# Dense feed-forwards: where the third weight split of a trip stands against the wait for the gate product

## The chip, the cores and the metric

The kernel runs on one core of a Trainium2 chip. The metric is the device time of one execution in microseconds (us). Everything is float32 at the interface; the kernel builds a float32 product out of three passes of a narrower format.

## The reference, cut to what matters

Two transformer blocks run one after the other on 256 tokens of width 1024. The first has two layers (mixer, cross-attention, convolutional feed-forward), the second has two layers (mixer, then a dense feed-forward in layer 0 and eight experts in layer 1). The change touches the three dense feed-forwards:

```
# first block, both layers: hidden width 2816, a 3-tap convolution along the tokens on the gate half
u, gt = split(x @ ffn_w_in);  a = dwconv(gt, conv_w) + conv_b
out = (silu(a) * u) @ ffn_w_out
# second block, layer 0: hidden width 3584
out = (silu(t @ w_gate) * (t @ w_up)) @ w_down
```

## The kernel before, in words

The hidden width is cut into pieces of 256 (`CW`): 11 trips in each feed-forward of the first block, 14 in that of the second. A trip `i` takes three weight chunks of 1 MB each (128 x 2048 values): gate(i), up(i) and down(i). Numbered in the order in which TensorE (PE) uses them they are gate(0), up(0), gate(1), up(1), down(0), gate(2), up(2), down(1), ... (`ffn_steps`), so that gate(i+1), up(i+1) and down(i) are the chunks 3i+2, 3i+3 and 3i+4, of 48 matmuls each.

Each chunk is split before use. ScalarE (ACT) copies the loaded float32 chunk into `w_hi`, rounded (the high part, L2132, `split_high`); VectorE (DVE) subtracts that from the chunk into `ring_low` (the low part, L1475, `split_low`). PE multiplies high by high, high by low and low by high. `w_hi` has four buffers: the high part of chunk c waits until PE has done the high passes of chunk c-4 (`ffn_done`, counted on the one matmul of a chunk that stands at L744). PE waits for the low part (`ffn_lo`) before each chunk.

Between the products, per trip: for the first block DVE applies the convolution to the gate product (`form`, L1700 to L1713); ACT takes the silu (`silu_of`; L2392 in the first block, L2413 in the second, where it waits for the gate product on PE and `form` does nothing); DVE multiplies silu and up product (L1488), ACT rounds the result into `act_hi` (L2235), DVE forms `act_lo` (L1490), and PE's down(i) uses both.

Every engine runs its instructions in the order in which they are written, and a wait holds all that is queued behind it on that engine. `dense_steps` writes the order out, once for ACT and once for DVE, with three calls of `split()` in a trip: for gate(i+1), up(i+1) and down(i). The first two chunks are split before it starts.

Each call of `split()` ends with `side(d)`, which hangs a piece of other work behind the d-th split: the weights of the modulation (`ada_w`, 24 chunks of 1 MB for each layer of the second block) are scaled on ACT (`scale_part`, 8 instructions, L2218) and added down from eight to one row block on DVE (`fold_down`, L1432 to L1436, one split later than on ACT). `due` spreads 12 of them over 28 splits in each feed-forward of the first block, and 24 over 36 splits in the second. There every trip has two on each engine: on ACT behind the splits of up(i+1) (scale A below) and of down(i) (scale B), on DVE behind the low parts of down(i) (fold A) and of the next gate chunk (fold B). The `ada_w` chunks pass through three buffers (`ring_tail`); GpSimd (POOL) fetches the next one when a fold has freed its buffer (L537).

The weight chunks pass through six buffers (`ring_head`); SyncE (SP) loads them, in the order up(i), gate(i), down(i-1), each when PE has left the buffer (L448).

Of the kernel before, what the change touches and what calls it, by code (L numbers as in the profile page):

```python
# [134 lines left out]
def program(nc, io):  # L135
# [3 lines left out]
    with ExitStack() as ctx:  # L139
# [115 lines left out]
        def ring(s):  # L255
            return ring_head[:, s, :] if s < 6 else ring_tail[:, s - 6, :]
# [124 lines left out]
        def due(d, folds):  # L381

            span = 28 if folds == 12 else 36
            return d * folds // span if 0 < d <= span else folds if d > span else 0
# [11 lines left out]
        def ffn_slot(i, n):  # L396

            if i == 3 * n - 1:
                return 3 * ((n - 1) % 2) + 2
            return (0, 1)[i] if i < 2 else (3, 4, 2, 0, 1, 5)[(i - 2) % 6]  # L400

        def ffn_low(i, n):

            return w_hi[:, (i + 1) % DEPTH_HI, :] if i == 3 * n - 1 else ring_low[:, ffn_slot(i, n), :]

        def dense_steps(split_of, form, finish, n, side):

            calls = [0]

            def split():  # L410

                if calls[0] < 3 * n - 2:
                    split_of(calls[0] + 2)
                    calls[0] += 1
                    side(calls[0])

            for i in range(n):
                form(i % 2, i)
                if i < n - 1:
                    split()  # L420
                finish(i % 2, i)
                if i < n - 1:
                    split()
                split()

        @block.sync
# [911 lines left out]
        def _(dve):  # L1338
# [4 lines left out]
            def pairs(b):  # L1343
                return tiles(bank[b][:, :], 2)
# [83 lines left out]
            def fold_down(n):  # L1428

                w = tiles(ring_tail[:, n % 3, :], KD)  # L1430
                dve.wait_ge(mod_scaled, n + 1)
                v.tensor_tensor(w[:, 0:4, :], w[:, 0:4, :], w[:, 4:8, :], ALU.add).then_inc(fold_step, 1)  # L1432
                dve.wait_ge(fold_step, 2 * n + 1)
                v.tensor_tensor(w[:, 0:2, :], w[:, 0:2, :], w[:, 2:4, :], ALU.add).then_inc(fold_step, 1)  # L1434
                dve.wait_ge(fold_step, 2 * n + 2)
                v.tensor_tensor(fold(n), w[:, 0, :], w[:, 1, :], ALU.add).then_inc(folded, 1)  # L1436
# [33 lines left out]
            def split_low(which, i, n, order=None):  # L1470

                dve.wait_ge(ffn_hi, ffn_base[which] + (i if order is None else order) + 1)
                if i == 3 * n - 1:
                    dve.wait_ge(ffn_done, ffn_base[which] + i + 2 - DEPTH_HI)
                v.tensor_tensor(ffn_low(i, n), ring(ffn_slot(i, n)), w_hi[:, i % DEPTH_HI, :].bitcast(F32), ALU.subtract).then_inc(ffn_lo, 1)  # L1475

            def dense(which, form, n, first, folds):

                def side(d):

                    for k in range(due(d - 2, folds), due(d - 1, folds)):
                        fold_down(first + k)

                def finish(p, i):

                    dve.wait_ge(up_full[p], f.next(up_full[p]))
                    dve.wait_ge(silu_ready[p], f.next(silu_ready[p]))
                    v.tensor_tensor(act[:, p, :, :], silu[:, p, :, :], pairs(2 * p + 1), ALU.mult).then_inc(f.count(product_ready[p]), 1)  # L1488
                    dve.wait_ge(act_hi_ready[p], f.next(act_hi_ready[p]))
                    v.tensor_tensor(act_lo[:, p, :, :], act[:, p, :, :], act_hi[:, p, :, :].bitcast(F32), ALU.subtract).then_inc(f.count(act_ready[p]), 1)  # L1490

                dense_steps(lambda i: split_low(which, i, n), form, finish, n, side)

            for j, tokens_in in enumerate((first_in, second_in)):
                dve.wait_ge(tokens_in, f.next(tokens_in, 16))
# [14 lines left out]
            for l in range(DEPTH):  # L1510
                with f.trip(LAYERS[l]):
# [13 lines left out]
                    for c in range(6):  # L1525
                        b, i = 4 if c == 5 else c % 4, c % 2
# [26 lines left out]
                    for u in range(18):  # L1553
# [31 lines left out]
                        if u >= 3 and u % 2 == 1:  # L1585
                            n = (u - 3) // 2
# [111 lines left out]
                    def form(p, i):  # L1698
# [13 lines left out]
                        for j in range(2):  # L1712
                            v.scalar_tensor_tensor(conva[:, p, j, 0:TOK - 1], g[:, j, 1:TOK], ffp[:, 4 * j + 2:4 * j + 3],  # L1713
                                                   conva[:, p, j, 0:TOK - 1], ALU.mult, ALU.add).then_inc(f.count(conv_ready[p] if j else vector_step), 1)

                    dense(l, form, FF1 // CW, 12 * l, 12)
                    if l + 1 < DEPTH:
                        low_part(l + 1, 0)
# [39 lines left out]
            for l in range(DEPTH):  # L1758
# [192 lines left out]
                if l == 0:  # L1951

                    dense(2, lambda p, i: f.bump(gate_full[p]), FF2 // CW, 24, 24)
                else:

# [161 lines left out]
        def _(eng):  # L2117
# [8 lines left out]
            def split_high(which, i, n):  # L2126

                s = ffn_slot(i, n)
                eng.wait_ge(ffn_loaded[s], f.next(ffn_loaded[s], 16))
                if i >= DEPTH_HI:  # L2130
                    eng.wait_ge(ffn_done, ffn_base[which] + i + 1 - DEPTH_HI)
                a.copy(w_hi[:, i % DEPTH_HI, :], ring(s)).then_inc(ffn_hi, 1)  # L2132
# [80 lines left out]
            def scale_part(n):  # L2213

                w = tiles(ring_tail[:, n % 3, :], KD)
                eng.wait_ge(ada_loaded[n % 3], 16 * (n // 3 + 1))
                for k in range(KD):
                    ins = a.activation(w[:, k, :], w[:, k, :], ACT.Copy, scale=cond[:, k:k + 1])  # L2218
                ins.then_inc(mod_scaled, 1)

            def dense(which, silu_of, n, first, folds):

                def side(d):

                    for k in range(due(d - 1, folds), due(d, folds)):
                        scale_part(first + k)

                downs = f.now(down_done)

                def finish(p, i):  # L2230
                    silu_of(p)
                    eng.wait_ge(product_ready[p], f.next(product_ready[p]))
                    if i >= 2:
                        eng.wait_ge(down_done, downs + i - 1)
                    a.copy(act_hi[:, p, :, :], act[:, p, :, :]).then_inc(f.count(act_hi_ready[p]), 1)  # L2235

                dense_steps(lambda i: split_high(which, i, n), lambda p, i: None, finish, n, side)
                f.bump(down_done, n - 1)

            def exps(u):  # L2240
# [30 lines left out]
            for l in range(DEPTH):  # L2271
                with f.trip(LAYERS[l]):
# [8 lines left out]
                    for u in range(18):  # L2281
                        if u < 16:
                            exps(u)
                        for k in fills(u):
                            b, i, c = 6 + k % 2, k % 2, 6 + k
# [107 lines left out]


                    dense(l, silu_conv, FF1 // CW, 12 * l, 12)
                    for i in range(3):
                        if l + 1 < DEPTH:
# [18 lines left out]
            for l in range(DEPTH):  # L2416
# [87 lines left out]
                if l == 0:  # L2504
                    biased(x_hi, mods[:, l, 24:32], x_hi_ready, x_hi_ready)
                    dense(2, silu_gate, FF2 // CW, 24, 24)
                    for i in range(3):
                        mixer_high(1, i)
# [199 lines left out]
```

## Time and profile before

| | us |
|---|---|
| median of the timed runs | 2760.72 (2759.31 to 2762.4, 3 runs) |
| span of the profiled execution, first to last instruction | 2760.0 |
| feed-forward of layer 0, first block | about 410 to 605 in the span |
| feed-forward of layer 1, first block | about 1000 to 1192 |
| dense feed-forward, second block | about 1342 to 1596 |

The profiled execution has no separate device time listed; its span stands 0.72 us below the median of the timed runs. In a timeline row the first number is the start in us from the span's beginning, the second the duration, then engine, line, operation, output<-inputs and count, and in brackets the idle time before it with what ended it. A row of waits reads: engine, waiting tile and line <- engine, tile and line that ended the wait: us in total, times, longest.

### The profile page before, as it was taken

The page shows a single profiled execution, that of the slowest core. Times are in us where ns is not written, and L with a number is a line of the kernel's source. Part 1 is how long each engine was busy: PE and PEld are TensorE (multiplying, and loading weights), DVE is VectorE, ACT ScalarE, POOL GpSimd, SP SyncE. Part 2 cuts the span into 40 slices and gives each one's busy share as a digit, 9 for nine tenths or more (in the row PEclk, how much of TensorE's full clock was granted, in tenths as well). Part 3 has the DMA queues.
Part 4 walks back from the last instruction along what each step waited for, and adds up shares of the span by engine and source line. Part 5 has one row for each costly group of instructions (what it writes and reads, how often), then busy time and mean ns, then how long its engine had stood idle before and what let it go on. Part 6 is the DMA issues. An engine that isn't in the chain of part 4 may idle for free.

```text
span 2760.0 us, 42476 instructions
## 1 busy us (share of the span) xinstructions
PE 2676.2 (97%) x18237; PEld 2463.7 (89%) x18245; DVE 2103.2 (76%) x2094; ACT 1683.0 (61%) x1817; POOL 71.6 (3%) x114
## 2 busy tenths in 40 slices
PE   7999999999999999999999999999999999999997
PEld 6999999999999999989899999888888888888886
DVE  6777658877667567867577666789898989888896
ACT  3555446654555456654577644677777777777775
POOL 1000000001000000000011000000000000000000
PEclk9999999999999999999999989999999999999999
DMA  8545548736445467543788733699989989998994
GB/s 258 167 144 167 164 163 274 266 126 186 143 137 185 153 234 269 200 120 100 245 295 295 235 92 93 259 373 356 376 342 364 367 348 369 347 385 339 361 368 181
DMA packets 303650, 679.20 MB, mean 246 GB/s; under 512 B 16576, under 2 KB 237024, under 8 KB 260320
## 3 DMA queue, kind: packets, MB, share of 16 engines
q1 hardware_dynamic: 288080, 617.67, 62.4%
q0 software_dynamic: 15376, 58.75, 6.5%
q8 instruction: 146, 2.39, 0.4%
q14 instruction: 48, 0.39, 0.0%
HBM read 675.32 MB, written 4.69 MB: 246 GB/s over the span
## 4 chain that ended last, share of the span: by engine, by line
PE 74%; DVE 11%; ACT 10%; issue 3%; DMA 2%; SPq 0%; POOL 0%; ACTq 0%; DVEq 0%
PE bank L579 71%; DVE ring_low L1475 3%; ACT w_hi L2132 3%; ACT ring_tail L2218 3%; DVE ring_tail L1432 1%; DMA ring_head<-in_w_in 1%; PE bank L1247 1%; DVE ring_low L1355 1%; DVE ring_tail L1434 1%; DMA ring_head<-in_ffn_w_in 1%; PE bank L665 1%; DVE gates L1488 1%; PE bank L682 1%; PE bank L622 1%; PE bank L724 0%
## 5 line engine op out<-in xcount | busy, mean ns | idle before, releaser
L1960 DVE TENSOR_TENSOR ew_lo<-ring_head,ew_hi 128x2048 fp32r<-128x2048 f32 x336 | 759.3, 2287 | 50.1 <-ACT ew_hi L2515 50.1
L2515 ACT CAST ew_hi<-ring_head 128x2048 fp32r<-128x2048 f32 x336 | 642.2, 1916 | 227.8 <-PE bank L579 227.8
L579 PE MATMUL bank<-xs_hi,ring_low 128*128 128x256 f32 (+1 forms) x2608 | 513.8, 284 | 2.6 <-DVE ring_low L1355 2.4
L579 PEld LDWEIGHTS bank<-xs_hi,ring_low 128*128 128x128 f32 (+1 forms) x2608 | 416.0, 190 | 4.6 <-DVE ring_low L1355 3.2
L579 PE MATMUL bank<-ew_hi,gathered_hi 128*128 128x512 f32 x896 | 353.7, 395 | 0.0
L579 PE MATMUL bank<-ew_hi,gathered_lo 128*128 128x512 f32 x896 | 349.5, 390 | 0.0
L579 PE MATMUL bank<-ew_lo,gathered_hi 128*128 128x512 f32 x896 | 348.9, 389 | 0.0
L579 PE MATMUL bank<-x_hi,w_hi 128*128 128x256 f32 x1152 | 319.6, 284 | 10.8 <-DVE ring_low L1475 7.6
L1475 DVE TENSOR_TENSOR ring_low<-ring_head,w_hi 128x2048 fp32r<-128x2048 f32 x105 | 239.8, 2289 | 101.4 <-ACT w_hi L2132 101.4
L579 PE MATMUL bank<-x_hi,ring_low 128*128 128x256 f32 x1152 | 314.7, 279 | 0.0
L579 PE MATMUL bank<-x_lo,w_hi 128*128 128x256 f32 x1080 | 294.8, 279 | 0.0
L579 PE MATMUL bank<-xs_lo,ring_low 128*128 128x256 f32 x958 | 265.0, 281 | 0.0
L579 PEld LDWEIGHTS bank<-x_hi,w_hi 128*128 128x128 f32 x1152 | 215.1, 190 | 16.0 <-DVE ring_low L1475 11.3
L2132 ACT CAST w_hi<-ring_head 128x2048 fp32r<-128x2048 f32 x108 | 203.3, 1903 | 25.7 <-DMA ring_head<-in_ffn_w_in 24.2
L579 PEld LDWEIGHTS bank<-x_hi,ring_low 128*128 128x128 f32 x1152 | 213.7, 188 | 0.0
L2146 ACT CAST ring_low<-ring_head 128x2048 fp32r<-128x2048 f32 (+1 forms) x82 | 142.3, 1739 | 116.5 <-PE bank L622 65.3
L579 PEld LDWEIGHTS bank<-ew_hi,gathered_lo 128*128 128x128 f32 x896 | 168.2, 188 | 35.9
L579 PEld LDWEIGHTS bank<-x_lo,w_hi 128*128 128x128 f32 x1080 | 200.1, 188 | 0.0
L1355 DVE TENSOR_TENSOR ring_low<-ring_head,ring_low 128x2048 fp32r<-128x2048 f32 (+1 forms) x82 | 170.0, 2079 | 38.4 <-ACT ring_low L2146 38.3
L579 PEld LDWEIGHTS bank<-ew_lo,gathered_hi 128*128 128x128 f32 x896 | 168.4, 188 | 33.5
L579 PEld LDWEIGHTS bank<-ew_hi,gathered_hi 128*128 128x128 f32 x896 | 168.3, 188 | 33.3 <-DVE ew_lo L1960 0.2
L579 PEld LDWEIGHTS bank<-xs_lo,ring_low 128*128 128x128 f32 x958 | 180.3, 190 | 0.5
(446 smaller groups left out, 5399.9 us busy)
## 6 DMA issues: line engine op xcount, KB each, us to landing
ring_head<-in_moe_w_gate SPq DMA_DIRECT2D x112, 1024.0 KB, 7.2
ring_head<-in_moe_w_up SPq DMA_DIRECT2D x112, 1024.0 KB, 7.0
ring_head<-in_moe_w_down SPq DMA_DIRECT2D x112, 1024.0 KB, 7.1
ring_head<-in_w_in SPq DMA_DIRECT2D x82, 1024.0 KB, 5.5
ring_tail<-in_ada_w POOLq DMA_DIRECT2D x48, 1024.0 KB, 10.2
ring_head<-in_ffn_w_in SPq DMA_DIRECT2D x44, 1024.0 KB, 7.2
ring_head<-in_ffn_w_out SPq DMA_DIRECT2D x22, 1024.0 KB, 8.9
ring_head<-in_xa_kv SPq DMA_DIRECT2D x16, 1024.0 KB, 5.7
```

The costliest lines, as they stand in the source:

```text
L579: ins = nc.tensor.matmul(out, lhsT, rhs, start=start, stop=stop, **kw)
L622: nc.tensor.matmul(out, lhsT, rhs, start=False, stop=False, skip_group_check=True).then_inc(chunk_done, 1)
L665: ins = nc.tensor.matmul(bank[at][:, 2 * (n - first) + j:2 * (n - first) + j + 1], fold(n)[:, j * P:(j + 1) * P], one, start=True, stop=True)
L682: ins = nc.tensor.transpose(out, src, ident)
L1247: ins = nc.tensor.transpose(both[:, j, :], eact[:, j * P:(j + 1) * P], ident)
L1355: v.tensor_tensor(ring_low[:, at, 0:n], ring(at)[:, 0:n], highs[i % 3][:, 0:n].bitcast(F32), ALU.subtract).then_inc(chunk_lo, 1)
L1475: v.tensor_tensor(ffn_low(i, n), ring(ffn_slot(i, n)), w_hi[:, i % DEPTH_HI, :].bitcast(F32), ALU.subtract).then_inc(ffn_lo, 1)
L1960: v.tensor_tensor(ew_lo[:, h, :], ring(c % 6), ew_hi[:, h, :].bitcast(F32), ALU.subtract).then_inc(w_used[c % 6], 1)
L2132: a.copy(w_hi[:, i % DEPTH_HI, :], ring(s)).then_inc(ffn_hi, 1)
L2146: a.copy(highs[i % 3][:, 0:n], ring(at)[:, 0:n]).then_inc(chunk_hi, 1)
L2218: ins = a.activation(w[:, k, :], w[:, k, :], ACT.Copy, scale=cond[:, k:k + 1])
L2515: a.copy(ew_hi[:, (e * len(PARTS) + c) % DEPTH_HI, :], ring(c % 6)).then_inc(f.count(part_hi), 1)
```

## The change

In `dense_steps` the function that was called once in a trip, `finish`, is cut in two: `middle`, which stays where it was, and a shorter `finish`, which moves behind the second split of the trip. For ACT `middle` is the silu, and `finish` is the wait for the product and the rounding into `act_hi`. For DVE `middle` does nothing and the whole of `finish` (product, `act_lo`) moves. So on both engines the split of up(i+1), chunk 3i+3, with the side work that hangs behind it, stands ahead of the product and of `act_hi` where it stood behind them. The last trip, which has one split only, is as before.

```diff
-        def dense_steps(split_of, form, finish, n, side):
+        def dense_steps(split_of, form, middle, finish, n, side):
...
                 form(i % 2, i)
                 if i < n - 1:
                     split()
-                finish(i % 2, i)
+                middle(i % 2)
                 if i < n - 1:
                     split()
+                finish(i % 2, i)
                 split()
...
-                dense_steps(lambda i: split_low(which, i, n), form, finish, n, side)
+                dense_steps(lambda i: split_low(which, i, n), form, lambda p: None, finish, n, side)
...
                 def finish(p, i):
-                    silu_of(p)
                     eng.wait_ge(product_ready[p], f.next(product_ready[p]))
                     if i >= 2:
                         eng.wait_ge(down_done, downs + i - 1)
                     a.copy(act_hi[:, p, :, :], act[:, p, :, :]).then_inc(f.count(act_hi_ready[p]), 1)
 
-                dense_steps(lambda i: split_high(which, i, n), lambda p, i: None, finish, n, side)
+                dense_steps(lambda i: split_high(which, i, n), lambda p, i: None, silu_of, finish, n, side)
```

## Rows read from the trace of the kernel before

**Rows 1.** The page, busy time by engine: us, share of the span, instructions.
```profile
PE 2676.2 (97%) x18237; PEld 2463.7 (89%) x18245; DVE 2103.2 (76%) x2094; ACT 1683.0 (61%) x1817; POOL 71.6 (3%) x114
```

**Rows 2.** The chain that ended last, 1340 to 1600: start, us, what.
```profile
1398.62 3.31 ACT ring_tail L2218 x8
...
1403.75 2.29 DVE ring_low L1475
```

**Rows 3.** Waits in 1360 to 1573: us in total, times, longest.
```profile
PEld bank L579 <- DVE ring_low L1475: 8.9, 12, 0.9
...
PE bank L579 <- DVE ring_low L1475: 6.5, 11, 0.7
```

**Rows 4.** Timeline of PE, second block: the L744 matmul marks a chunk's end.
```profile
1366.12 0.28 PE L744 MATMUL bank<-x_lo,w_hi 128*128 128x256 f32 x1
...
1377.32 0.28 PE L744 MATMUL bank<-x_lo,w_hi 128*128 128x256 f32 x1
...
1378.35 0.39 PE L579 MATMUL bank<-x_hi,w_hi 128*128 128x256 f32 x1 [0.65 <-DVE ring_low L1475]
...
1383.88 0.28 PE L744 MATMUL bank<-x_lo,w_hi 128*128 128x256 f32 x1
...
1578.77 0.28 PE L744 MATMUL bank<-x_lo,w_hi 128*128 128x256 f32 x1
```

**Rows 5.** Timeline of ACT over one trip (i = 2) of the second block.
```profile
1384.08 1.91 ACT L2132 CAST w_hi<-ring_head 128x2048 fp32r<-128x2048 f32 x1
1385.88 0.60 ACT L2413 ACTIVATE gates<-bank 128x512 f32<-128x512 f32 x1
1391.28 0.62 ACT L2235 CAST act_hi<-gates 128x512 fp32r<-128x512 f32 x1 [4.79 <-DVE gates L1488]
1391.80 1.91 ACT L2132 CAST w_hi<-ring_head 128x2048 fp32r<-128x2048 f32 x1
1393.62 3.30 ACT L2218 ACTIVATE ring_tail<-ring_tail,cond 128x256 f32<-128x256 f32 x8
1396.82 1.90 ACT L2132 CAST w_hi<-ring_head 128x2048 fp32r<-128x2048 f32 x1
1398.62 3.31 ACT L2218 ACTIVATE ring_tail<-ring_tail,cond 128x256 f32<-128x256 f32 x8
1401.82 1.90 ACT L2132 CAST w_hi<-ring_head 128x2048 fp32r<-128x2048 f32 x1
```

**Rows 6.** Timeline of DVE over the same trip.
```profile
1386.03 2.29 DVE L1475 TENSOR_TENSOR ring_low<-ring_head,w_hi 128x2048 fp32r<-128x2048 f32 x1 [0.40 <-ACT w_hi L2132]
1388.24 1.22 DVE L1432 TENSOR_TENSOR ring_tail<-ring_tail 128x1024 f32<-128x1024 f32 x1
...
1390.56 0.68 DVE L1488 TENSOR_TENSOR gates<-gates,bank 128x512 f32<-128x512 f32 x1
...
1393.74 2.29 DVE L1475 TENSOR_TENSOR ring_low<-ring_head,w_hi 128x2048 fp32r<-128x2048 f32 x1 [1.12 <-ACT w_hi L2132]
1398.75 2.29 DVE L1475 TENSOR_TENSOR ring_low<-ring_head,w_hi 128x2048 fp32r<-128x2048 f32 x1 [2.71 <-ACT w_hi L2132]
```

**Rows 7.** Transfers, second block: SP and POOL issues; us to landing (last number).
```profile
1384.84 0.58 SPq L448 DMA_DIRECT2D ring_head<-in_ffn_w_gate  x1
...
1390.94 0.88 POOL L537 DMA_DIRECT2D ring_tail<-in_ada_w  x1 [4.13 <-DVE gates L1436]
...
ring_head<-in_ffn_w_gate SPq DMA_DIRECT2D x12, 1024.0 KB, 12.1
...
DMA to landing us min/median/max: 9.3/10.6/11.6
```

**Rows 8.** First block: PEld waits (layer 0, layer 1), and 45 us by engine.
```profile
PEld bank L579 <- DVE ring_low L1475: 0.9, 2, 0.6
...
PEld bank L579 <- DVE ring_low L1475: 0.6, 2, 0.3
...
435.00:480.00 45.00, 45.00 (x388) 45.00 (x387) 36.38 (x41) 31.13 (x46) 3.32 (x4) 1.00 0.83 280
```
In the last row the columns are: span, length, then busy us (and instructions) of PE, PEld, DVE, ACT and POOL, granted clock, DMA share, GB/s.

## The prediction

> **What bounds the kernel now.** I read the page's busy times first: PE is the busiest engine at 97% [rows 1], so a change of order among ACT and DVE can only give back the few per cent in which PE stands. The next question is where PE stands because of the code that moves. The waits of PE, stretch by stretch, answer it: in the dense feed-forward of the second block PE's weight loads wait 12 times for the low part of a chunk, never more than 0.9 us [rows 3]; in the two feed-forwards of the first block they do so twice each, for 0.9 and 0.6 us in all [rows 8]. So the second block is the place.
>
> There the markers of the chunk ends on PE give the size [rows 4]. From up(1), at 1366.12, two chunks take 11.20 us, 5.60 each. The following one, up(2), ends 6.56 after its predecessor, and its first matmul waited for the low part. From the end of up(1) to that of up(13), at 1578.77, there are 36 chunks, 12 trips: 212.65 us, where 36 x 5.60 would be 201.60. A trip takes 17.72 us against 16.80 that PE needs; the loss is 11.05 us, about 0.92 in a trip. I read the markers of all 36: the long interval is always the one of an up chunk, the third in splitting order, 0.75 to 0.97 over 5.60 and 10.6 in all; the other 0.45 is spread over chunks of 5.65.
>
> The chain that ended last says why: in this stretch it runs through ACT and DVE, not PE, with the second scaling of a trip and then the low part of the gate chunk on it [rows 2]. It is a loop, and the two timelines let it be added up, start to start [rows 5, 6]. From the start of the gate split on ACT (1384.08): 1.95 to the low part on DVE, 4.53 to the product (low part, then fold B), 0.72 to act_hi, 0.52 to the split of up, 1.82 to scale A, 3.20 to the split of down, 1.80 to scale B, 3.20 to the next gate split: 17.74, the period that PE shows. In that loop ACT stands 4.79 us before act_hi with nothing to do, while the split of up, whose data are there, is queued behind that wait.
>
> **The change part by part.** No instruction is added or removed; the ACT split of up(i+1) with scale A goes ahead of the product wait and of act_hi, the DVE low part of up(i+1) goes ahead of the product and act_lo. No DMA instruction moves. SP's loads follow PE, POOL's fetches follow the folds.
>
> *The second block, 12 trips.* The new loop, from the gate split on ACT: 1.95 to its low part, 4.53 over low part and fold B; now the low part of up comes, one such instruction start to start, 2.21 (1386.03 to 1388.24); product at 8.69. Then 0.72 to act_hi and 0.52 to the split of down: 9.93; 1.80 to scale B: 11.73; 3.20 to the next gate split: 14.93 us [rows 5, 6]. That is 2.8 less than now, since the split of up and scale A (1.82 + 3.20 = 5.02) leave the loop and 2.21 enters it. It is under PE's 16.80 by 1.87, so PE is late next, and the trip becomes 16.80.
>
> Two arms could be longer. On ACT: gate split 1.80, silu 0.60, up split 1.82, scale A 3.20, done at 7.42, ahead of act_hi at 9.41: scale A costs nothing, hidden by DVE's low parts and fold; if that cover went, ACT's own sum (7.42 + 0.52 + 1.80 + 3.20 = 12.94) would still be under 16.80. On DVE the low part of up now stands ahead of the product and can hold product, act_lo and through them act_hi; it is wanted at 1.95 + 4.53 = 6.48, the split of up ends by 4.3, so it does not wait. The split of up waits for the high passes of gate(i); silu, just ahead of it, waits for the whole of gate(i), so that wait adds nothing. Its load stands ahead of the gate load in SP's order, and the gate split ran already.
>
> The gain there lies between the idle time of the weight loads, 8.9 us [rows 3], and the whole distance to 5.60 per chunk, 11.05 [rows 4]. I take 11.0, since the markers measure PE's rate itself.
>
> The Trainium skill (Trace Analysis, Identifying the Most-Contended Engine) holds matmul busy time for a bad measure of PE, because matmuls are pipelined, and wants the busy time of the weight loads. The rows bear that out: the same stalls are 6.5 us as idle time before matmuls and 8.9 before weight loads [rows 3], and by the first the gain here would be 6.5, by the second 8.9; the chunk markers give 11.05, more than either.
>
> *The product comes later.* It moves back by 2.21 us against the gate split in every trip. PE needs act_hi and act_lo for down(i), which comes after gate(i+1) and up(i+1): two chunks, 11.2 us after up(i), from which the product is taken. In the new loop the low part of down(i) starts 1.93 after its split (1396.82 to 1398.75), at 11.86, and ends at 14.1, while PE's chunks are taken at its own pace. Cost nothing; without that cover it would be 2.21 x 12 = 27 us.
>
> *Loads.* The gate load is issued 0.96 us after the end of up(2) (1383.88 to 1384.84) and lands in 12.1 [rows 4, 7]. PE comes to that chunk, gate(4), four chunks after, at 22.4. After landing it needs 1.95 + 2.2, so 17.2 of 22.4: it may delay ACT's gate split within the slack, not PE.
>
> *The first block, 22 trips.* DVE is busy 36.38 of 45 us and ACT 31.13 [rows 8]; the shift of the product meets the same 11.2 us of lead. What can be won is 0.9 + 0.6 [rows 8], what can be lost nothing as long as that lead holds. I take 1.5: where scaling hangs on the up split, ACT did it behind act_hi while DVE waited, as in rows 6 (2.71 us of idle before the low part of down); it now runs during DVE's low parts.
>
> Sum: 11.0 + 1.5 = 12.5 us. What follows a feed-forward is ordered by PE's end, so it moves forward whole. The profiled span is 2760.0, the median 2760.72; taken from the median, 2748.2. The forecast's own range is 2746 to 2752 (8.9 alone at the upper end, some 2 us for the runs at the lower).
>
> **The rivals.**
>
> *The fetch of the modulation weights takes the place of the stall.* With three buffers and two folds in a trip, fold A of trip i frees the buffer for scale B of trip i+1. From a gate split, fold A ends at 11.86 + 2.21 + 2.32 = 16.39 [rows 5, 6]; the fetch is issued at most 0.38 later (1390.56 to 1390.94) and takes F to land, 9.3 to 11.6 now [rows 7]; scale B takes 3.20 and ends at the gate split of trip i+2. So 16.39 + 0.38 + F + 3.20 = 19.97 + F must fit into two trips. At F = 11.6 it is 31.6, under 33.6: no stall. From F = 13.6 it binds. At 14.7 the trip is 17.3 and the gain 12 x 0.4 + 0.5 = 5.3: 2755.4. For it: the trips follow each other faster, so the five transfers of 1 MB in each lie closer. Against it: the longest F seen is 2.0 short of the point.
>
> *The same, to the other side: slower.* From F = 15.5 the trip is longer than today's 17.72, and scale B, in front of the gate split on ACT, holds everything behind it. At F = 17.5 the trip is 18.7, 12 x 1.0 = 12 us more: 2772.7. It would take fetches half as long again as the longest of now.
>
> On this the Trainium skill (DMA: Bandwidth & Descriptors, Queues, rings and completion order) says that each DMA engine takes turns between the queues that have work, packet by packet. By that rule a fetch shares with SP's loads and does not stand behind all of them, which would keep F near the 11.6 seen and the slower case out; no row shows a denser stage, so my chance keeps it.
>
> *It does not do what it says:* the split of up is held by something else, its load or its buffer, and runs no earlier. Then 2760.7. The 4.79 us in which ACT stood before act_hi, with the split following 0.52 after it without any further wait [rows 5], speak against it.
>
> **How the numbers follow.** Forecast 0.80, the fetch with part of the gain 0.10, no effect 0.06, slower 0.04. The time is the forecast's, 2748.2. The range goes from 2745.5 to 2757, over the partial case. About 0.2%, 5.5 us, is what a measurement can tell from no change: faster means under 2755.2. The forecast and six tenths of the partial case are there: 0.86; same 0.10; slower 0.04.
>
> **What would show it.** In the changed profile the markers of the second block should stand 5.60 apart through all chunks (up(1) to up(13) in 202 us), the waits of PE and PEld for L1475 be gone there, ACT's order be gate split, silu, up split, scaling, act_hi, with a wait before act_hi of some 2 to 5 us, and the chain through this stretch run on PE. Idle time on ACT before L2218 ended by a load of ada_w would show the fetch rival. The prediction is wrong if the trip stays over 17.3, or if the first block's waits for L1475 grow.

## The result, and the profile after

The changed kernel takes 2745.88 us (median of 5 runs, 2743.82 to 2750.63), the kernel before 2759.70 beside it (5 runs, 2759.04 to 2762.40). The ratio is 0.9948, with a 95% interval of 0.9936 to 0.9959: 14.4 us less, between 11.3 and 17.7. The forecast was 12.5 less, which lies in that interval. By the ratio, taken from 2759.70, the time is 2745.4, a hair under the lower end of the range (2745.5); taken from the 2760.72 of the forecast it is 2746.4, inside, and the median alone lies 0.4 above that end. Repeated in a later series, the changed kernel took 2744.82 and the ratio was 0.9949 [0.9935, 0.9963].

Both kernels issue 42476 instructions. The page of the changed kernel, busy time by engine, against [rows 1]:

```profile
PE 2672.4 (97%) x18237; PEld 2462.2 (90%) x18245; DVE 2103.2 (77%) x2094; ACT 1684.5 (61%) x1817; POOL 71.7 (3%) x114
```

No engine does less; the span is 2748.6, 11.4 under that of before. The Trainium skill (Perfetto Trace Analysis, Identifying the Most-Contended Engine) holds that matmul busy time is not a good measure of how close PE is to its limit, and the trace agrees: PE stands at 97% in both kernels. The weight loads, which it names instead, go from 89% to 90%.

What has changed is on the chain that ended last. The changed kernel, 1335 to 1600 (start, us, what), against [rows 2]:

```profile
1393.19 5.54 PE bank L580 x47
...
1398.84 5.54 PE bank L580 x47
```

Where before the chain ran through the second scaling and the low part of the gate chunk, it now goes from one PE chunk to the next; ACT and DVE are off it all through the loop. The lines of the changed kernel stand one further on: L580, L745, L1476, L1489, L2133, L2219 answer to L579, L744, L1475, L1488, L2132, L2218.

The waits in 1360 to 1573 (us in total, times, longest), against [rows 3]:

```profile
DVE ring_low L1476 <- ACT w_hi L2133: 38.4, 24, 3.8
ACT act_hi L2235 <- DVE gates L1489: 32.8, 13, 5.8
ACT w_hi L2133 <- DMA ring_head<-in_ffn_w_gate: 19.3, 8, 3.3
```

The waits of PE and PEld for L1476 are not there at all. What remains are ACT and DVE waiting for each other, and ACT for the gate load: waits of engines that are not the bound.

PE's chunk markers, first up(1), last up(13) and then the last two chunks of the feed-forward, against [rows 4]:

```profile
1364.64 0.28 PE L745 MATMUL bank<-x_lo,w_hi 128*128 128x256 f32 x1
...
1568.16 0.28 PE L745 MATMUL bank<-x_lo,w_hi 128*128 128x256 f32 x1
1573.82 0.28 PE L745 MATMUL bank<-act_lo,w_hi 128*128 128x256 f32 x1
1583.25 0.28 PE L745 MATMUL bank<-act_lo,w_hi 128*128 128x256 f32 x1
```

203.52 us for the 36 chunks, where before took 212.65. All are 5.65 long, not one stalls; but 5.65 is not the 5.60 of [rows 4], and the last chunk takes 9.43. Both matter below. The same markers in a second profile of the changed kernel, label e7_after_again:

```profile
1360.63 0.28 PE L745 MATMUL bank<-x_lo,w_hi 128*128 128x256 f32 x1
...
1562.23 0.28 PE L745 MATMUL bank<-x_lo,w_hi 128*128 128x256 f32 x1
1567.83 0.28 PE L745 MATMUL bank<-act_lo,w_hi 128*128 128x256 f32 x1
1575.67 0.28 PE L745 MATMUL bank<-act_lo,w_hi 128*128 128x256 f32 x1
```

Here the 36 chunks take 201.60, exactly 36 x 5.60, and the last one 7.84.

A trip on ACT after the change, against [rows 5]:

```profile
1378.24 1.90 ACT L2133 CAST w_hi<-ring_head 128x2048 fp32r<-128x2048 f32 x1
1380.04 0.59 ACT L2413 ACTIVATE gates<-bank 128x512 f32<-128x512 f32 x1
1380.53 1.91 ACT L2133 CAST w_hi<-ring_head 128x2048 fp32r<-128x2048 f32 x1
1382.33 3.31 ACT L2219 ACTIVATE ring_tail<-ring_tail,cond 128x256 f32<-128x256 f32 x8
1387.62 0.62 ACT L2235 CAST act_hi<-gates 128x512 fp32r<-128x512 f32 x1 [1.98 <-DVE gates L1489]
1388.14 1.91 ACT L2133 CAST w_hi<-ring_head 128x2048 fp32r<-128x2048 f32 x1
1389.96 3.30 ACT L2219 ACTIVATE ring_tail<-ring_tail,cond 128x256 f32<-128x256 f32 x8
1396.51 1.91 ACT L2133 CAST w_hi<-ring_head 128x2048 fp32r<-128x2048 f32 x1 [3.25 <-DMA ring_head<-in_ffn_w_gate]
```

The split of up and scale A fill most of the idle time before act_hi. The last row shows an engine that has become free: ACT waits 3.25 us for the gate load, a wait that the trip of [rows 5] does not have.

The transfers: the gate loads in 1350 to 1580 (last number: median us to landing), against [rows 7].

```profile
ring_head<-in_ffn_w_gate SPq DMA_DIRECT2D x12, 1024.0 KB, 10.6
```

And the fetches of the modulation weights in 1360 to 1573:

```profile
DMA to landing us min/median/max: 5.7/8.2/11.2
```

They land earlier than before, 8.2 against 10.6 in the median, though the trips follow each other faster.

### The profile page after: what moved, and what is told of

It is laid out like the page before. It is cut to its first block, busy times and chain, and to the rows that moved or that the text cites. A ratio compares the mean times of both kernels' runs of the same rounds, so it can differ in the third digit from the quotient of the medians.

```text
span 2748.6 us, 42476 instructions
## 1 busy us (share of the span) xinstructions
PE 2672.4 (97%) x18237; PEld 2462.2 (90%) x18245; DVE 2103.2 (77%) x2094; ACT 1684.5 (61%) x1817; POOL 71.7 (3%) x114
## 4 chain that ended last, share of the span: by engine, by line
PE 89%; DVE 4%; ACT 3%; DMA 2%; issue 1%; SPq 0%; POOL 0%; DVEq 0%; ACTq 0%
PE bank L580 86%; DMA ring_head<-in_w_in 1%; PE bank L1248 1%; DVE ring_low L1356 1%; PE bank L666 1%; PE bank L623 1%; PE bank L683 1%; DMA ring_head<-in_w_mix_out 0%; PE bank L725 0%; PE bank L745 0%; ACT ring_low L2147 0%; DMA ring_head<-in_ffn_w_in 0%; ACT chunk_high L2147 0%; DVE ring_low L1476 0%; ACT chunk_high L2161 0%
## 5 line engine op out<-in xcount | busy, mean ns | idle before, releaser
L580 PE MATMUL bank<-xs_hi,ring_low 128*128 128x256 f32 (+1 forms) x2608 | 513.6, 284 | 2.6 <-DVE ring_low L1356 2.4
L580 PEld LDWEIGHTS bank<-xs_hi,ring_low 128*128 128x128 f32 (+1 forms) x2608 | 415.9, 190 | 4.5 <-DVE ring_low L1356 3.2
L580 PE MATMUL bank<-ew_hi,gathered_hi 128*128 128x512 f32 x896 | 353.6, 395 | 0.0
L580 PE MATMUL bank<-ew_hi,gathered_lo 128*128 128x512 f32 x896 | 349.5, 390 | 0.0
L580 PE MATMUL bank<-ew_lo,gathered_hi 128*128 128x512 f32 x896 | 349.0, 390 | 0.0
L580 PE MATMUL bank<-x_hi,w_hi 128*128 128x256 f32 x1152 | 316.9, 281 | 2.9 <-ACT x_hi L2211 2.6
L580 PE MATMUL bank<-x_hi,ring_low 128*128 128x256 f32 x1152 | 316.2, 280 | 0.0
L1476 DVE TENSOR_TENSOR ring_low<-ring_head,w_hi 128x2048 fp32r<-128x2048 f32 x105 | 240.2, 2289 | 75.6 <-ACT w_hi L2133 75.6
L580 PE MATMUL bank<-x_lo,w_hi 128*128 128x256 f32 x1080 | 295.4, 280 | 0.0
L580 PE MATMUL bank<-xs_lo,ring_low 128*128 128x256 f32 x958 | 264.8, 281 | 0.0
L2133 ACT CAST w_hi<-ring_head 128x2048 fp32r<-128x2048 f32 x108 | 205.2, 1906 | 62.6 <-DMA ring_head<-in_ffn_w_in 42.0
L580 PEld LDWEIGHTS bank<-x_hi,w_hi 128*128 128x128 f32 x1152 | 215.3, 190 | 4.5 <-issue 3.0
L580 PEld LDWEIGHTS bank<-x_hi,ring_low 128*128 128x128 f32 x1152 | 213.5, 188 | 0.0
L580 PEld LDWEIGHTS bank<-ew_hi,gathered_lo 128*128 128x128 f32 x896 | 168.1, 188 | 35.8
L580 PEld LDWEIGHTS bank<-x_lo,w_hi 128*128 128x128 f32 x1080 | 199.9, 188 | 0.0
L580 PEld LDWEIGHTS bank<-ew_lo,gathered_hi 128*128 128x128 f32 x896 | 168.5, 188 | 33.5
L580 PEld LDWEIGHTS bank<-ew_hi,gathered_hi 128*128 128x128 f32 x896 | 168.3, 188 | 33.5 <-DVE ew_lo L1961 0.2
L580 PEld LDWEIGHTS bank<-xs_lo,ring_low 128*128 128x128 f32 x958 | 180.2, 190 | 0.5
```

Source lines behind the costliest of these rows:

```text
L580: ins = nc.tensor.matmul(out, lhsT, rhs, start=start, stop=stop, **kw)
```

## The experiments

Each kernel ran beside the kernel before on the same chip; a ratio is to that kernel, an interval is 95%.

**The new order in the second block alone** (`e1_second_only`).

```diff
+            early = n == FF2 // CW
...
                 middle(i % 2)
+                if not early:
+                    finish(i % 2, i)
                 if i < n - 1:
                     split()
-                finish(i % 2, i)
+                if early:
+                    finish(i % 2, i)
```

> The new order in the dense feed-forward of the second block alone; the two of the first block as before. If the gain is the ACT and DVE loop of the second block: trips there of 3 PE chunks (16.8 to 17.0 us, by whether PE takes a chunk in 5.60 or 5.65), no wait for the low part, and 9 to 11 us less than before, some 2749 to 2751. If the first block brings as much as the second, half of what the change brought: about 2753.

2746.66 (5 runs), ratio 0.9952 [0.9938, 0.9965]: 13.2 us less, between 9.7 and 17.1. Up(1) to up(13), timeline of PE:

```profile
1368.91 0.28 PE L749 MATMUL bank<-x_lo,w_hi 128*128 128x256 f32 x1
...
1570.51 0.28 PE L749 MATMUL bank<-x_lo,w_hi 128*128 128x256 f32 x1
```

201.60, and the last chunk took 7.84. One feed-forward carries the whole gain that can be measured; it is more than the 9 to 11 us that were expected of it.

**The new order in the first block alone** (`e2_first_only`): the same edit with `early = n != FF2 // CW`.

> The new order in the two feed-forwards of the first block alone. By the loop of the second block as cause: trips there stay at 17.7 us, and the first block gives what its waits for low parts were, 1 to 2 us: about 2758 to 2760. If what the prediction left out lies in the first block, over 2.5 us less than before: below 2757.

2759.08 (11 runs), ratio 0.9999 [0.9990, 1.0008]: no change, within 2.8 us. The waits of PE for low parts are gone from both feed-forwards of the first block, and it brings nothing that the runs resolve. In the second block the loop of before is back, 212.68 from up(1) to up(13):

```profile
1363.66 0.28 PE L749 MATMUL bank<-x_lo,w_hi 128*128 128x256 f32 x1
...
1576.34 0.28 PE L749 MATMUL bank<-x_lo,w_hi 128*128 128x256 f32 x1
```

**The split of up ahead, but its scaling left behind act_hi** (`e3_scale_behind`). `hold` is true for ACT in the second block's feed-forward; `split(False)` leaves the side work to the later call.

```diff
                 if i < n - 1:
-                    split()
+                    split(not hold)
                 finish(i % 2, i)
+                if i < n - 1 and hold:
+                    side(calls[0])
                 split()
```

> As the changed kernel, but in the second block scale A goes back behind act_hi on ACT; only the split of up stays ahead of the wait. By the loop sum from the rows of before: product at 8.69 us after the gate split, act_hi 9.41, scale A 9.93 to 13.13, split of down to 14.93, scale B to 18.13: a trip of 18.1 us, longer than the 17.72 of before, so the second block loses 12 x 0.4 = 5 us and the whole is 2762 to 2765. If the split of up is what mattered (its low part being ready early for PE), the stall stays away: trips of 16.8 to 17.0 and 2746 to 2748.

2758.68 (11 runs), ratio 0.9991 [0.9982, 1.0000]. The split of up is as early as in the changed kernel, and nearly the whole gain is gone. ACT over one trip:

```profile
1477.65 1.89 ACT L2136 CAST w_hi<-ring_head 128x2048 fp32r<-128x2048 f32 x1
1479.45 0.58 ACT L2416 ACTIVATE gates<-bank 128x512 f32<-128x512 f32 x1
...
1487.02 0.62 ACT L2238 CAST act_hi<-gates 128x512 fp32r<-128x512 f32 x1 [5.19 <-DVE gates L1492]
1487.55 3.30 ACT L2222 ACTIVATE ring_tail<-ring_tail,cond 128x256 f32<-128x256 f32 x8
1490.76 1.90 ACT L2136 CAST w_hi<-ring_head 128x2048 fp32r<-128x2048 f32 x1
1492.55 3.30 ACT L2222 ACTIVATE ring_tail<-ring_tail,cond 128x256 f32<-128x256 f32 x8
1495.76 1.90 ACT L2136 CAST w_hi<-ring_head 128x2048 fp32r<-128x2048 f32 x1
```

From gate split to gate split without any wait for data other than the product: 18.11 us, which is the changed kernel's 14.93 with the 3.20 of scale A put back. PE now stands at the down chunk:

```profile
1446.15 0.28 PE L748 MATMUL bank<-act_lo,w_hi 128*128 128x256 f32 x1
...
1458.79 0.39 PE L583 MATMUL bank<-act_hi,w_hi 128*128 128x256 f32 x1 [1.04 <-DVE ring_low L1479]
...
1464.27 0.28 PE L748 MATMUL bank<-act_lo,w_hi 128*128 128x256 f32 x1
```

Its trips are 18.12 long where the loop binds. There are nine of these stalls (1.32 more per trip), not twelve, so the 36 chunks took 213.99, only 1.3 over the kernel before, and the last chunk took 7.84; the time is below the 2762 to 2765 that were expected.

**Only the scaling ahead, the split of up behind as before** (`e4_scale_only`), in the second block: the order of before on both engines, and ACT does scale A ahead of the wait for the product.

```diff
                 middle(i % 2)
+                if i < n - 1 and hold:
+                    side(calls[0] + 1)
...
                 finish(i % 2, i)
+                if i < n - 1 and old:
+                    split(not hold)
```

> In the second block the order of before on both engines, except that on ACT scale A goes ahead of the wait for the product while the split of up stays behind act_hi; the first block as changed. By the loop sum 17.74 - 3.20 = 14.54 us, under three chunks: no stall, trips of 16.8 to 17.0 us, and the time of the changed kernel, 2744 to 2749. If the split of up has to move, trips stay at 17.7 and the time is 2757 to 2760.

2746.70 (5 runs), ratio 0.9952 [0.9939, 0.9966]: as good as the changed kernel. ACT over a part of a trip:

```profile
1481.11 0.58 ACT L2419 ACTIVATE gates<-bank 128x512 f32<-128x512 f32 x1
1481.59 3.30 ACT L2225 ACTIVATE ring_tail<-ring_tail,cond 128x256 f32<-128x256 f32 x8
1486.48 0.62 ACT L2241 CAST act_hi<-gates 128x512 fp32r<-128x512 f32 x1 [1.59 <-DVE gates L1495]
1487.01 3.71 ACT L2139 CAST w_hi<-ring_head 128x2048 fp32r<-128x2048 f32 x2
1490.63 3.30 ACT L2225 ACTIVATE ring_tail<-ring_tail,cond 128x256 f32<-128x256 f32 x8
```

The splits of up and of down stand together behind act_hi (x2). PE has no stall; its chunks are 5.60 apart, but for one of 5.72. With the run before, this tells the two halves of the move apart as far as they were tried: the 3.20 us of scaling ahead is enough by itself, and the split ahead is not, where DVE's low part of up goes ahead too. Not tried is the split alone with DVE's order left. By the sum that loop is 17.74 - 1.82 = 15.92, also under 16.80, so it is not shown that the scaling has to move.

**ACT's order changed, DVE's left** (`e5_act_only`), in all three feed-forwards.

```diff
-                dense_steps(lambda i: split_low(which, i, n), form, lambda p: None, finish, n, side)
+                dense_steps(lambda i: split_low(which, i, n), form, lambda p: None, finish, n, side, False)
```

Here the last argument, `early`, is the switch of the first experiment.

> ACT in the changed order in all three feed-forwards, DVE in the order of before (product and act_lo ahead of the low part of up). By the loop sum: gate split 0, product at 6.48, scale A done at 7.42, so act_hi at 7.42, split of down 7.94, scale B 9.74, next gate split 12.94 us: under three chunks, trips of 16.8 to 17.0, no wait of PE for a low part, ACT no longer idle before act_hi by more than what PE's pace leaves, and the time of the changed kernel, 2744 to 2749. If DVE's reorder carries a part of the gain, trips lie between 17.0 and 17.7 and the time between 2750 and 2758.

2743.60 (5 runs), ratio 0.9947 [0.9934, 0.9961], the same as the changed kernel beside it on that chip (2744.82). DVE's half of the change carries nothing. The waits in 1360 to 1573:

```profile
ACT w_hi L2136 <- DMA ring_head<-in_ffn_w_gate: 39.5, 11, 5.3
```

By the sums the product is 2.2 us earlier without DVE's low part of up in front and ACT's loop 2.0 shorter (12.94 for 14.93), and all it gains is a longer wait for the gate load, 39.5 us against 19.3. The other half, DVE's move without ACT's, cannot run: DVE's low part of up would wait for a split that ACT does only behind the product, and the product would wait behind that low part.

**The fetch of the modulation weights one fold later** (`e6_two_buffers`), in the second block: in effect two buffers in place of three.

```diff
-                if n >= first + 3:
-                    pool.wait_ge(folded, n - 2)
+                ahead = 2 if first == 24 else 3
+                if n >= first + ahead:
+                    pool.wait_ge(folded, n + 1 - ahead)
```

> The changed kernel, but in the second block the fetch of a modulation chunk waits one fold longer, as if there were two buffers and not three: this makes the fetch the last link on purpose. Then fold A of a trip frees scale A of the next, and one trip holds scale A 3.20, act_hi 0.52, split of down to its low part 1.93, low part 2.21, fold 2.32, issue 0.38 and the landing F: 10.56 + F. With F of 8 to 11 us trips of 18.6 to 21.6, some 20 to 50 us over the changed kernel (2765 to 2800), and ACT idle before L2219 ended by the load. If the scaling were not on the path, no change: 2744 to 2749.

2782.02 (4 runs), ratio 1.0085 [1.0069, 1.0100]: 37 us over the changed kernel on that chip. The 36 chunks took 236.37, 19.7 a trip; by the sum that is a landing of 9.1 us, and the fetches in 1360 to 1573 took 9.7 in the median. The waits in 1360 to 1585, and after them ACT's timeline:

```profile
ACT ring_tail L2220 <- DMA ring_tail<-in_ada_w: 74.8, 18, 8.3
...
PEld bank L581 <- DVE ring_low L1477: 24.6, 13, 4.6
```

```profile
1480.09 0.59 ACT L2414 ACTIVATE gates<-bank 128x512 f32<-128x512 f32 x1
...
1488.80 3.31 ACT L2220 ACTIVATE ring_tail<-ring_tail,cond 128x256 f32<-128x256 f32 x8 [6.33 <-DMA ring_tail<-in_ada_w]
1492.01 0.60 ACT L2236 CAST act_hi<-gates 128x512 fp32r<-128x512 f32 x1
```

So the rival of the prediction is a real mechanism: a scaling whose load is late holds act_hi and everything behind it. With three buffers it does not bind: the changed kernel's list of waits has no such row. It is not far off, though: where only the scaling went ahead, ACT waits for a fetch twice, 1.4 us in all.

**Both kernels again.** The profiles disagreed on two small things that the prediction had not counted, the length of a chunk (5.60 or 5.65) and that of the last chunk, so there are four profiles of each kernel. First:

> The changed kernel once more, for its profile and for the size of the gain. In the profiles so far PE takes a chunk of a dense feed-forward in 5.60 or in 5.65 us, and keeps one of the two until it is interrupted. If that is a draw per execution and not the change's doing, this profile should show 5.60 in at least one of the three feed-forwards (the first profile of it had 5.65 in all), and the time 2743 to 2750. If the change itself costs PE its pace, 5.65 in all three again.

> The kernel before once more, for a second profile: trips of the second block at 17.72 us whatever the pace (the loop sets them), the stalls of the up chunks 0.92 long at a pace of 5.60 and 0.77 at 5.65; in the first block stalls of some tenths only where the pace is 5.60.

Then:

> The changed kernel, a third profile, for what the prediction's sum left out. In four profiles with no stall in the second block and PE at 5.60 us a chunk, the last chunk (down(13), with the modulation products ahead of it) took 7.84 us at a granted clock of 1.00; with the stalls of before it took 9.39 at 0.89. If the stalls go with that fall of the clock: 7.84 to 7.88 here wherever the second block runs at 5.60. If it is a draw: 9.4 about as often.

> The same, a fourth profile: pace 5.60 or 5.65 in each feed-forward, the last chunk 7.84 with 5.60; span between 2738 and 2749.

> The kernel before, a third profile: 212.6 us from up(1) to up(13) of the second block at either pace, and the last chunk at 9.4 us if the fall of the clock belongs to the stalls, 7.84 in some profiles if it is a draw.

> The same, a fourth profile of the kernel before: 212.6 us, last chunk 9.4; span between 2753 and 2762.

All times in us, from each profile's span and its markers; the feed-forward is counted from the marker of gate(0) to that of its last chunk.

| profile | span | up to gate(0) | the feed-forward | after it | up(1) to up(13) | last chunk |
|---|---|---|---|---|---|---|
| before | 2760.0 | 1349.0 | 244.8 | 1166.2 | 212.65 | 9.39 |
| before, e8_before_again | 2754.4 | 1343.1 | 244.9 | 1166.4 | 212.61 | 9.39 |
| before, e11_before_third | 2760.0 | 1349.1 | 244.8 | 1166.1 | 212.63 | 9.38 |
| before, e12_before_fourth | 2758.0 | 1347.3 | 244.8 | 1165.9 | 212.65 | 9.42 |
| changed | 2748.6 | 1347.6 | 235.7 | 1165.3 | 203.52 | 9.43 |
| changed, e7_after_again | 2741.1 | 1343.7 | 232.0 | 1165.4 | 201.60 | 7.84 |
| changed, e9_after_third | 2739.6 | 1342.5 | 232.0 | 1165.1 | 201.6 | 7.83 |
| changed, e10_after_fourth | 2742.7 | 1345.6 | 231.9 | 1165.2 | 201.6 | 7.83 |

By the means of these profiles the changed kernel is 15.1 us shorter: 11.9 in the dense feed-forward of the second block, 2.3 ahead of it, 0.9 behind it. Of the three parts only the first is clear. What stands ahead of gate(0) took 1342.4 to 1353.1 over the profiles of all kernels here, and the longest, 1352.0 and 1353.1, are one with the old order of the first block and one with the new. The 2.3 can be placed: 0.8 lies in the first 32 chunks of the two feed-forwards of the first block, and the rest, some 1.5, in their last chunks. Those took 9.6, 11.2 or 12.8 us in profiles of either order, by how long the clock was low in them, so that part is not shown to be the change's.

## Why the prediction was right in kind and short in size

**What bounds the kernel, and the loop: right.** The loop of 17.74 set the trip: the 36 chunks take 212.61 to 212.65 in all four profiles of the kernel before, though the chunks between the stalls are 5.60 long in some and 5.65 in others. PE's own pace made no difference as long as the loop was longer. (The split that moves, that of up(i+1), is the second of the three in a trip; the title and the prediction call it the third.)

**The new loop: right to 0.03 us.** From the gate split at 1378.24 act_hi starts at 9.38 (9.41 summed), the split of down at 9.90 (9.93), scale B at 11.72 (11.73). PE is late next, as said; 36 chunks take 201.6 in three of four profiles (202 forecast). The wait before act_hi is 1.98 in the trip shown, 2.5 in the mean of 13. The gate load does delay ACT's gate split, by up to 3.3 us, and PE never sees it.

**Which part of the change does it: not separated in the prediction.** It counted 1.82 + 3.20 out of the loop and 2.21 in. The two runs that took the move apart show that the 3.20 alone suffices: with scale A behind act_hi, and DVE's 2.21 in the loop, the loop is 18.11; with only scale A ahead PE never stalls. Whether the 1.82 of the split would suffice without the 2.21 no run shows. DVE's reorder, the 2.21, is a cost within the slack.

**The later product: right.** It costs nothing; the run without it gains nothing.

**The fetch rival: its premise was wrong.** It expected the fetches to take longer to land when trips follow each other faster. They took 8.2 in place of 10.6 in the median, and the longest is 11.2, below the 11.6 of before and far from 13.6. The Trainium skill (DMA: Bandwidth & Descriptors, Queues, rings and completion order) has each DMA engine take turns between the queues that have work, packet by packet. The trace agrees in that a fetch need not wait for the loads issued before it: in the changed kernel one issued at 1418.29 landed at 1427.91, ahead of a gate load issued at 1416.48, which landed at 1429.06.

**The size: the term that failed is the second block's 11.0.** The prediction held the gain there to lie between 8.9 and 11.05. That counted the 36 chunks between up(1) and up(13) and put what stands outside them at nothing, without a reason. The feed-forward as a whole goes from 244.8 to 232.0, 12.8 us, in three of the four profiles of the changed kernel (11.9 in the mean of all four). Of the 12.8, 11.05 are the 36 chunks, as the markers had it; 1.56 are the last chunk, down(13), from 9.39 to 7.83, and the other 0.2 stand ahead of up(1). The windows view over that chunk and some of the one ahead of it says what it is (span, length, busy us and instructions of PE, PEld, DVE, ACT, POOL, granted clock, DMA share, GB/s); the kernel before:

```profile
1578.00:1594.00 16.00, 16.00 (x127) 16.00 (x127) 10.71 (x11) 10.77 (x9) 0.00 (x0) 0.89 0.31 77
```

and the changed kernel, label e7_after_again:

```profile
1562.00:1576.00 14.00, 14.00 (x124) 14.00 (x122) 10.62 (x11) 10.15 (x8) 0.00 (x0) 1.00 0.34 87
```

The same chunk, and a granted clock of 0.89 against 1.00: with 2.4 GHz at 1.00, the first stretch ran in part at the lower level, 1.2 GHz. The trace of before had that row, and the prediction never asked for it. It would not have told which way the clock goes after the change, but it would have put 1.6 us into the bounds.

What the clock follows is settled only in part. The last chunk opens with 20 matmuls of one column each, the modulation products (PE's timeline, kernel before). Behind them the clock is at the lower level (windows view):

```profile
1584.61 2.29 PE L665 MATMUL bank<-const,gates 128*128 128x1 f32 x20
```

```profile
1588.00:1591.00 3.00, 3.00 (x16) 3.00 (x15) 2.07 (x3) 2.24 (x2) 0.00 (x0) 0.50 0.00 0
```

Whether it falls there goes neither with the stalls nor with the order, but with the time from the marker of gate(0) to that of down(12), where the last chunk begins. Over all 14 profiles (us):

| gate(0) to down(12) | profiles | last chunk |
|---|---|---|
| 224.1 to 224.5 | six without stalls at 5.60 (e1, e4, e5, e7, e9, e10) | 7.83 to 7.89 |
| 226.3 | the first of the changed kernel: no stall, 5.65 | 9.43 |
| 235.4 to 235.5 | four of the kernel before, and e2: twelve stalls | 9.38 to 9.42 |
| 236.7 | e3: nine stalls | 7.84 |
| 259.1 | e6: waits for fetches | 9.40 |

Loops of nearly equal length ended alike each time. So the 1.56 follows from how long the loop became, and that it came out as a gain is luck: at the pace of 5.65 the stalls were gone as well, and the clock fell all the same. Why one length ends with a fall and another without stays open.

**The first block's 1.5: not there, or too small to see.** The stalls went, as forecast; the run of that part alone gives 0.9999 [0.9990, 1.0008]. A feed-forward there is 173.7 us from its first chunk to its 32nd when PE draws 5.60 and 175.4 when it draws 5.65; in the kernel before it was 174.8 to 175.4. The draw is worth as much as the stalls were, and the mean of the four profiles is 0.8 shorter for both feed-forwards together.

**The range.** Its lower end allowed 2 us for the runs. The spans of the four profiles of each kernel are 5.6 and 9.0 apart, and the interval of the ratio is over 6 us wide. What is clear of the gain is 12.8 in the one feed-forward, or 9.1 where PE drew the longer pace; with up to 0.9 behind it that makes some 10 to 14. The measured 11.3 to 17.7 does not ask for more, and whether the parts ahead of the feed-forward add to it stays open. That the time came out at the very end of the range, on one side of it by the ratio and on the other by the median, is within these draws.

## What to carry to other kernels

When a stall comes from a loop through two engines, add the loop up start to start, and look for a long piece of work in it that hangs on nothing in the loop: here 3.20 us of side work was enough by itself, and it could have moved without the split it was attached to. Take such a piece out where an engine waits ahead of it, and check by the same sum that the bound becomes another engine. When a stage is sized by equal intervals, read the uneven one at its end too, with its granted clock, and give the range the spread that several profiles show and not that of three runs.

## What the runs showed of the hardware that was not expected

PE runs the same 48-matmul chunk in 5.60 or in 5.65 us (117 or 118 ns a matmul), both at a granted clock of 1.00. One feed-forward without stalls keeps one of them throughout; in the kernel before both occur within a feed-forward, on either side of a stall. The four profiles of the changed kernel drew, for its three dense feed-forwards, 5.65 in all; 5.60, 5.65, 5.60; 5.60 in all; and 5.65, 5.60, 5.60. For 36 chunks that is 1.9 us. What decides it no run here shows.

The 1 MB fetches of the stage landed sooner in shorter trips, not later: medians in 1360 to 1573 of 7.7 to 8.7 us in the seven profiles without stalls, against 10.6 to 10.8 in the five with the stalls of before. The gate loads show it less (9.7 to 12.1 against 11.4 to 12.2), the up loads not at all (5.1 to 7.3 against 5.1 to 5.2). Why, no run here shows.
